# Order of VectorE's work in the odd mixing phase, unread products on TensorE, and stores of zeros per block

## The reference, cut to what matters

```python
def odd_layer(h, s_gdn, s_conv, norm_w, w_in, conv_w, a_log, dt_bias, gn_w, w_out):
    p = jnp.einsum('bld,de->ble', rmsnorm(h, norm_w), w_in)
    qkv, z, b_raw, a_raw = jnp.split(p, ...)
    xp = jnp.concatenate([s_conv, qkv], axis=1)
    qkv = jax.nn.silu(sum(xp[:, j:j + L] * conv_w[j] for j in range(GDN_CONV)))
    ...
    o, s_gdn_new = gated_delta_chunked(q, k, v, beta, g, s_gdn)
    o = (head_rmsnorm(o) * gn_w).reshape(B, L, O_MIX) * jax.nn.silu(z)
    out = o @ w_out
    return h + out.astype(h.dtype), s_gdn_new, xp[:, -(GDN_CONV - 1):]
```

## Time and profile before

| | us |
|---|---|
| median of 3 runs | 3169.6 (3165.99 to 3186.61) |
| profiled execution | 3168.01 |
| its span, first to last instruction | 3166.2 |
| TensorE busy | 2978.1 (94%) |
| VectorE busy | 1864.6 (59%) |
| ScalarE busy | 1032.0 (33%) |
| GpSimd busy | 502.9 (16%) |

### The profile page before, as it was taken

The page is one execution under the profiler, slowest core; times in us unless marked ns, Lnnn a source line. Parts: engine busy times, 40 slices in busy tenths (PEclk is TensorE's granted clock), DMA queues, the critical chain, the costliest instruction groups (busy, mean ns, idle before and its releaser), DMA issues. The chain is left out here.

```text
span 3166.2 us, 88698 instructions
## 1 busy us (share of the span) xinstructions
PE 2978.1 (94%) x38430; PEld 2714.3 (86%) x38430; DVE 1864.6 (59%) x3858; ACT 1032.0 (33%) x2337; POOL 502.9 (16%) x519
## 2 busy tenths in 40 slices
PE   8999999994899999999969999999995899999998
PEld 8999999993788888888769999999995788888886
DVE  4311222324677777777535156777665778887876
ACT  4211111113333443343157122222223344444441
POOL 0000000001333433333300000000001111111112
PEclk9999999996799999999889999999997899999998
DMA  5321212115233333343353221222114223333333
GB/s 166 99 73 60 73 64 69 67 49 170 71 97 115 120 111 118 112 126 122 100 176 110 75 69 61 74 75 70 66 47 158 72 82 96 95 96 95 94 98 127
DMA packets 222915, 302.15 MB, mean 95 GB/s; under 512 B 32184, under 2 KB 163520, under 8 KB 222528
## 3 DMA queue, kind: packets, MB, share of 16 engines
q1 hardware_dynamic: 213376, 266.54, 26.1%
q0 software_dynamic: 9152, 29.94, 3.0%
HBM read 200.70 MB, written 95.71 MB: 94 GB/s over the span
## 5 line engine op out<-in xcount | busy, mean ns | idle before, releaser
L363 DVE SCALAR_TENSOR_TENSOR po_stage<-po_work,po_cw,po_stage 128x424 f32<-128x424 f32 (+1 forms) x360 | 232.1, 645 | 27.6 <-issue 0.9
L476 PE MATMUL po_ps<-po_xnT_hi,po_w_hi 128*128 128x424 f32 x960 | 205.0, 355 | 0.0
L476 PE MATMUL po_ps<-po_xnT_hi,po_w_lo 128*128 128x424 f32 x960 | 204.4, 355 | 0.0
L476 PE MATMUL po_ps<-po_xnT_lo,po_w_hi 128*128 128x424 f32 x960 | 204.1, 354 | 0.0
L270 ACT ACTIVATE po_work<-po_ps 128x424 f32<-128x424 f32 (+1 forms) x120 | 61.6, 514 | 408.3 <-PE po_ps L476 408.3
L476 PEld LDWEIGHTS po_ps<-po_xnT_hi,po_w_hi 128*128 128x128 f32 x960 | 180.2, 188 | 5.2
L476 PEld LDWEIGHTS po_ps<-po_xnT_hi,po_w_lo 128*128 128x128 f32 x960 | 180.4, 188 | 4.5
L476 PEld LDWEIGHTS po_ps<-po_xnT_lo,po_w_hi 128*128 128x128 f32 x960 | 180.2, 188 | 4.6
L476 PE MATMUL pe_ps<-pe_w_hi,pe_xnT_hi 128*128 128x256 f32 x1088 | 154.9, 285 | 4.3 <-DVE pe_w_lo L382 3.6
L476 PE MATMUL pe_ps<-pe_w_lo,pe_xnT_hi 128*128 128x256 f32 x1088 | 153.4, 284 | 0.0
L476 PE MATMUL pe_ps<-pe_w_hi,pe_xnT_lo 128*128 128x256 f32 x1088 | 152.7, 283 | 0.0
(11 more groups left out here) (453 smaller groups left out, 7169.3 us busy)
## 6 DMA issues: line engine op xcount, KB each, us to landing
me_ring<-scratch_w_lo SPq DMA_DIRECT2D x68, 512.0 KB, 3.8
mo_c<-scratch_ch_o SPq DMA_DIRECT2D x51, 512.0 KB, 3.5
scratch_ch_o<-po_stage SPq DMA_DIRECT2D x96, 212.0 KB, 1.9
scratch_tok_e<-pe_stage SPq DMA_DIRECT2D x136, 128.0 KB, 1.9
pe_raw<-in_w_in_e POOLq DMA_DIRECT2D x52, 256.0 KB, 3.7
me_xs<-scratch_ch_e SPq DMA_DIRECT2D x17, 768.0 KB, 6.2
po_raw<-in_w_in_o POOLq DMA_DIRECT2D x48, 256.0 KB, 3.8
scratch_ch_e<-pe_stage SPq DMA_DIRECT2D x52, 212.0 KB, 1.9
```

The source lines that it names most:

```text
L363: return nc.vector.scalar_tensor_tensor(out=o, in0=a, scalar=s, in1=b, op0=op0, op1=op1)
L476: last = nc.tensor.matmul(out, left.bitcast(F32R), right.bitcast(F32R), start=(i == 0 and k == 0), stop=(i == 2 and k == KD - 1))
```

## The change

Four edits, none of which changes a result:

- `project_phase`: the two stores of zeros of a block are issued by SyncE behind the store of that block's first product, and no longer all ahead of the fourth tile's load.
- `mix_odd_phase`, VectorE: the mask of level 16 stands ahead of `normed` and `mixed`; `final_norm` stands ahead of `outputs`; the splits of weights 4 to 7 are spread over the step with `n` = 1, as those of 0 to 3 already are over the step with `n` = 0.
- both mixing phases, TensorE: `keep_clock(count)` makes `count` products of the identity with itself (128x128) into a bank that holds nothing at that time and whose content nobody reads. They stand in the steps with `m` = 0, `n` = 0 and `n` = 1. The even phase has 29 around tile 0's turning (`m` = 0), 36 more with `n` = 0, and 34 in each of the two steps with `n` = 0 and 1; the odd phase has 9, 14 and 44 in each.

```diff
@@ project_phase, sync
             sp.wait_ge(s_zero, 1)
-            for b in range(ch_blocks):
-                sp.dma_start(ch_out[:, b, 0:FRONT], zero[:, 0:FRONT]).then_inc(s_zst, 16)
-                sp.dma_start(ch_out[:, b, FRONT + SEQ + NS:], zero[:]).then_inc(s_zst, 16)
             for n, (u, what) in ORDER:
...
                 sp.dma_start(dst, stage[j][:, 0:w]).then_inc(s_st[j], 16)
+                if what[0] != "tok" and what[2] == 0:
+                    sp.dma_start(ch_out[:, b, 0:FRONT], zero[:, 0:FRONT]).then_inc(s_zst, 16)
+                    sp.dma_start(ch_out[:, b, FRONT + SEQ + NS:], zero[:]).then_inc(s_zst, 16)
@@ mix_even_phase, tensor (and the same helper in mix_odd_phase)
+            def keep_clock(count):
...
+                for _ in range(count):
+                    mm(BC[0][:, 0:P], ident, ident)
...
+                if n == 0:
+                    keep_clock(8)
                 if n is not None:
                     level_X(n, 2)
...
+                if n == 0:
+                    keep_clock(12)
                 if n is not None:
                     level_T(n, 2)
...
                     project(p, 0)
+                elif p is None and n is not None:
+                    keep_clock(4)
...
+                if m == 0:
+                    keep_clock(24)
                 if m is not None:
                     turn_factors(m)
@@ mix_odd_phase, vector
                 if n is not None:
                     mask(n, 2)
-                    if n == 0:
-                        split_weights(0)
+                    if n < 2:
+                        split_weights(4 * n)
...
                 if n is not None:
                     mask(n, 4)
-                    if n == 0:
-                        split_weights(1)
+                    if n < 2:
+                        split_weights(4 * n + 1)
+                if o is not None and p != PT:
+                    final_norm(o)
                 if t is not None:
                     outputs(t)
...
                 if n is not None and n < 2:
-                    split_weights(2 if n == 0 else 4)
+                    split_weights(4 * n + 2)
...
-                if o is not None and p != PT:
-                    final_norm(o)
                 if n is not None:
                     turn_blocks(n, 8)
+                    mask(n, 16)
+                    if n < 2:
+                        split_weights(4 * n + 3)
                 if t is not None:
                     normed(t)
-                if n is not None:
-                    mask(n, 16)
-                    if n == 0:
-                        split_weights(3)
-                if t is not None:
                     mixed(t)
-                if n == 1:
-                    for k in range(5, KD):
-                        split_weights(k)
@@ mix_odd_phase, tensor
                 if t is not None:
                     state_products(t)
+                if n == 0:
+                    keep_clock(14)
                 if n is not None:
                     level_X(n, 2)
...
                     project(p, 0)
                     project(p, 1)
+                elif p is None and n is not None:
+                    keep_clock(6)
...
                     project(p, 6)
                     project(p, 7)
+                elif p is None and n is not None:
+                    keep_clock(22)
```

More of the change, by code:

```diff
@@ L1946, in _ @@
                     project(p, 6)
+                elif p is None and n is not None:
+                    keep_clock(4)
                 if t == PT:
                     sample_wk_state(1)
+                if m == 0:
+                    keep_clock(5)
                 if m is not None:
@@ L2826, in turn, with keep_clock @@
                 return nc.tensor.transpose(o, i, ident)
+            def keep_clock(count):
+                for _ in range(count):
+                    mm(bk[BC[0]][:, 0:P], ident, ident)
             def state_products(t):
```

## The result

| | before | changed |
|---|---|---|
| median of the runs, us | 3168.12 (4 runs, 3165.99 to 3186.61) | 3130.16 (4 runs, 3126.73 to 3134.26) |
| ratio, 95% interval | | 0.9871 (0.9852 to 0.9889) |
| profiled span, us | 3166.2 | 3132.5 |
| TensorE busy, us | 2978.1 | 3007.9 |

The account below looks back on a forecast made before the run. TensorE was taken as the bound, busy 94% of the span, losing time at phase starts, where its clock falls, and in waits on VectorE. Terms 12 + 21 + 20 = 53 us: 3168.0 - 53 + 1.6 = 3117 us, range 3098 to 3142.

Parts of the forecast that it names:

- Zeros per block: Odd projection: tile 3's load no longer queues behind 48 stores of zeros; 9.27 us of waiting and 2.7 us of clock, 12 us.
- Masks ahead of norms: Steady steps of the odd mixing phase: TensorE's waits on VectorE's `mo_XA` go; bounds 18 and 22.5, taken as 21 us.
- Unread products, even phase: Start of the even mixing phase: added products keep TensorE's clock full; 6.5 and 7.2 us less in two windows.
- four fifths: Share taken of the 25.7 us for unread products in both mixing phases, as the clock may hold less well: 20 us.
- Unread products, odd phase: Start of the odd mixing phase: added products keep the clock full; 7.1, 3.5 and 1.4 us less, before four fifths.
- full clock all through: Starts of both mixing phases: case where the clock never falls, leaving only waits on other engines; 25.7 us less.
- Weights' splitting: Odd mixing phase, VectorE: spreading splits of weights 4 to 7 adds 0; a split beside GpSimd may take 1.5 us more.
- products at the old clock: Starts of both mixing phases: if the clock averaged as before, products take 53 us against 31.6 of idling; 21.8 us more.
- The first: Rival: clock still falls at the mixing phases' starts; 3137 us with nothing won (chance 0.10), 3159 with a loss (0.05).
- The second: Rival: in steady odd steps VectorE is late at level 32's mask or the outputs instead; 3138 us, chance 0.06.
- the third: Rival: in the odd projection tile 3 is late anyway, for instance behind the raw weights' loads; 3126 us, chance 0.04.
- the fourth: Rival: slower, as the final norm ahead of outputs waits for ScalarE's root; 3192 us at 5 us late, chance 0.03.

## Why the prediction came out as it did, point by point

**Zeros per block, 12 us.** Right: 11.9 us in the changed kernel's odd projection, 11.7 alone. Nothing was lost by the two stores behind each block; TensorE waits for no buffer there.

**Masks ahead of norms, 21 us.** Right in mechanism and size, by itself: 19 us over the whole, 23.4 in the phase. Four profiles (of three kernels) with the new order and no fill took 733.1, 739.9, 730.3 and 734.4 us in the phase, in the mean 734.4, which is 22 less than 756.5. In the changed kernel the twelve steady steps give 12 us (470.1 against 482.2) and not 21, since 6.3 us of breaks at borders have taken the place of 18 us of waits; in the profiles without fill these breaks were 1.9 to 7.9 us. A steady step was forecast at 38.3 us; undisturbed ones take 38.4.

**Unread products, even phase.** The forecast was 6.5 + 7.2 us in the two windows; 14 us over all profiles, with the clock at 0.98 and 1.00. Right; taking four fifths was not needed here. The 24 products ahead of tile 0's factors cost nothing:

```profile
741.15 8.57 PE L1567 MATMUL me_b<-me_ident 128*128 128x128 f32 x48 [4.59 <-DMA me_blocks<-in_blocks_e]
751.09 0.44 PE L1570 MATMUL me_b<-me_ident,me_BK 128*128 128x128 f32 x2 [1.36 <-DVE me_KR L1207]
```

They waited 4.59 us for a table and were done at 749.72, and the transposes behind them waited another 1.36 us for VectorE's `me_KR`. That these began at 751.09 and not at 750.10 us, as before, is VectorE's; in the changed kernel's second profile they began at 750.21 us, after 2.69 us of waiting.

**Unread products, odd phase.** This is the step that failed. The prediction put 7.1, 3.5 and 1.4 us, times four fifths: about 9 us. In their place the start became 6.6 us longer than before (174.9 against 168.3; 171.8 in the second profile), and the new order alone had made it 4.8 us shorter. The sum assumed that at full clock TensorE would be idle only where another engine was late ("full clock all through"). Two things in it were wrong. First, TensorE can also wait for its own instructions, at a border of 256: 12.9 us in this start, where the order alone has 3.7. The products that were to fill the gaps put 444 instructions more into it and took away the waits in which packets could come; how much of this is their number and how much the place of the borders stays open. Second, three such breaks of 1.5 to 2.8 us at this start were followed by the clock's fall, and then the following 7 us and more of real products ran at half. So the clock averaged 0.90 over the start, not 1.00. The waits on other engines that the prediction said would stay were sized about right (7.6 us in its two windows, 5.5 measured in the whole start). The trace of before had a sign of it, the 1.32 us in a level's product at 2443.98 us that nothing ended, and I did not ask what it was.

**Weights' splitting.** Right that it moves nothing of the sum that the traces show. The split that shares its time with GpSimd took 1.71 us and the others 1.22:

```profile
2444.72 1.90 POOL L2302 TENSOR_TENSOR mo_gm<-mo_gm,mo_ba 128x1024 f32<-128x1024 f32 x1 [7.84 <-DVE mo_TA L2721]
...
2445.99 1.71 DVE L2529 TENSOR_TENSOR mo_w_lo<-mo_mix,mo_w_hi 128x1024 fp32r<-128x1024 f32 x1
...
2451.50 1.21 DVE L2529 TENSOR_TENSOR mo_w_lo<-mo_h,mo_w_hi 128x1024 fp32r<-128x1024 f32 x1
```

The Trainium skill ("GPSIMD Engine Reference", section 1) has VectorE's instructions with two SBUF inputs contend with GpSimd; the trace agrees, but with 0.5 us for this split and not the 1.5 us of the earlier trace rows. In both cases the extra time is close to what GpSimd's instruction had left when the split began: 2446.62 - 2445.99 = 0.63 us here, 2436.82 - 2435.18 = 1.64 us in the earlier trace rows.

**The sum.** 12 + 21 + 20 = 53 became 11.9 + 14.6 + 7.2 = 33.7 in the profiled spans and 38 in the medians. The missing 30.3 - 7.2 = 23 us are 16 at the odd phase's start (6.6 longer, not 9.3 shorter) and 9 in its steady steps (21 - 12.1), less 1.7 at its end. (The 21.8 us that the prediction has for products at the old clock are 53.1 - 31.6 = 21.5.) The total stayed in its range because that range left room for starts that give nothing; no second error made up for the first.

**The rivals.** The first, that the clock still falls, is what happened, in the odd phase alone; its reason there (waits for VectorE's longer work) holds for one of the stretches at half clock only, the 6.9 us behind the first block transpose; idle times at the start other than at borders are 5.5 us in all. The second did not happen (no wait on a later mask), nor the third, nor the fourth (no wait of VectorE ahead of `mo_h`).

## What to carry to other kernels

Before work is put into gaps to keep a clock up, count its instructions as well as its time: the same columns in a third of the instructions, with the borders moved by that, made this start 17 to 20 us shorter. When an idle time ends with no releaser, count the records between two of them; if they stand a fixed number apart, look whether the supply of instructions comes in pieces of that number, for then an edit far upstream can move the breaks. And profile a phase twice before a difference of 10 us in it is explained: one kernel gave 739.9 and 730.3 us here.

## What the runs showed of the hardware that I had not expected

- TensorE's instructions arrive in packets of 16 KB, 256 instructions; where TensorE waits for one, it goes on 2.16 us or more after the packet's start (median 2.42, 139 times), and at none of 4293 borders earlier than 2.16 us behind it. No packet started before TensorE was within 300 instructions of the border. Half a block of 32x32 products is executed in 0.75 us.
- The idle time at a border was up to 3.3 us, and 3 to 19 us in all over one odd mixing phase. What makes a packet start late beyond that was not tried. Loads alone do not: the share of the transfer engines was 0.99 in the last 0.6 us of the break at 2468.56 us, and 0.00 in that at 2671.86 us.
- A plain fp32 product with 128x128 weights takes 0.43 us for 8 columns at the phase's start, at granted clock 0.50, so it is no cheap filler; one with 32x32 weights took 6.50 / 59 = 0.11 us there.
- Two kernels with the same instructions in a phase differed by 18 us in it (730.8 and 749.3 us), and two executions of one kernel by 10 (739.9 and 730.3 us). Comparisons of edits worth less than 1% of this kernel need the phases looked at one by one.
